# Four pieces instead of two begun tile by tile, with their low halves taken for both tiles at once

## The chip, the cores and the metric

One core of one Trainium2 chip runs the whole program. The metric is the device time of one execution in microseconds. Three runs of the kernel before gave a median of 1691.17 us (1690.84 to 1694.19).

## The reference, cut to what matters

The program computes three transformer layers over 256 tokens of width 1024, in float32. Three places in it matter here, and they have the same shape: a norm over the width, and right behind it a projection of all 256 normed tokens.

```
# layer 1, second half: PEER (product-key experts)
xn = rmsnorm(h, norm2_g)
q  = (xn @ w_q).reshape(n_tok, 8, 2, 128)         # 16 pieces of 128 columns
sc = einsum("thpk,hpnk->thpn", q, sub_keys)       # scores against 128 keys, then top 16 ...

# layers 2 and 3, second half: feed-forward with a short convolution (D_FF = 2816 = 22 chunks of 128)
h  = layer_norm(DEEPNORM_ALPHA * h + y, ln1_g, ln1_b)
gate, up = split(h @ w_in, 2)
gate = conv3(gate, conv_w) + conv_b
f  = (silu(gate) * up) @ w_out
```

## The kernel before, in words

**Numbers in two parts.** TensorE (PE) multiplies in a rounded 32-bit format. Each float32 operand is split: the high half is the value rounded by a copy on ACT, the low half is what is left, by a subtraction on DVE (`take_high` L807, `take_low` L1709 for a weight piece of 128x1024; L826 or L830 and L1722 or L1733 for the activations). A product is high x high + high x low + low x high.

**Pieces.** A projection of the normed tokens is cut into pieces of 128 output columns. A piece has 8 weight blocks of 128x128, one per 128 features (`k`). The result stands transposed, 128 columns by 256 tokens, in one PSUM bank of 512 columns. Weight pieces pass through a ring of four slots: SP loads `raw`, ACT makes `high`, DVE makes `low`, and PE frees the slot (`slot_done`).

**Three ways to do one piece.** `project_in` (L1244): three matmuls of 256 columns per `k` (L1240 to L1242), the sum complete in 256 PSUM columns. `project_in_halves` (L1256): the high weights against `[xh | xl]` as one matmul of 512 columns (L1260), then the low weights against `xh`, 256 columns (L1262); the two 256-column halves of the bank must be added later. `project_in_tile` (L1265): the same for one tile of 128 tokens; the high weights with 256 columns (L1273), the low weights with 128 columns (L1274). Two tiles make a piece, 32 matmuls.

**The norm and the projection meet.** The token tiles (0 and 1, 128 tokens each) leave the norm one after the other on DVE. `turn` (L1224) transposes a tile by 128x128 blocks (L1230), four blocks to a quarter; quarters 0 and 1 are tile 0, quarters 2 and 3 are tile 1, and quarter `n` lands in bank `4 + n`. ACT reads a quarter into `xh`, DVE makes `xl` from the bank and `xh` and raises `xT_ready`. `turn` of tile 0 is followed by `keep_warm` matmuls (L1236). Then, at all three places, PE's order is: piece 0 tile 0, `turn` of quarters 2 and 3, piece 1 tile 0, piece 0 tile 1, piece 1 tile 1. Each `k % 4 == 0` waits for its quarter. Behind that come two more pieces as a whole: queries 2 and 3 by `project_in` (L1352), or the gate and up pieces of chunk 1 by `project_in_halves` (`gate_and_up` L1674).

**What follows in the queries.** DVE adds the halves of queries 0 and 1 (L1967), then makes `xf` (L1971); ACT copies queries 2 and 3 out (L920). PE computes the scores of the four queries (L1361, 16 matmuls, banks 0 and 1), in order of the queries, then expert blocks (L1373).

**What follows in a feed-forward.** For chunk 0: ACT copies the gate's low-half sum (L1187), DVE adds the other half and does the convolution (L2395 to L2398), ACT applies Silu (L1190, after loading its table), ACT and DVE bring the `up` piece (L1192, L2405), DVE multiplies (L2407), ACT and DVE split the product into `yh` and `yl` (L1198, L1722). In between, both engines split weight pieces for the ring (`ahead`). PE then multiplies by the output weights (`project_out`, L1290 to L1294), which waits for `hid_low`, the signal of `yl`. In DVE's written order, `layer_norm` (L1794) ends with the low halves of quarters 2 and 3 and, behind them, the low halves of the two weight pieces of chunk 1 (`take_low`, L1812); only then comes chunk 0's `hidden`. The high halves of these two pieces are made early, ahead of tile 0's quarters (`norm`, L798). For the queries the order is the same: quarters 2 and 3 (L1961), then the low halves of queries 2 and 3.

Everything is in the written order of each engine; nothing is planned at run time.

## Time and profile before

| | |
|---|---|
| median of three runs | 1691.17 us |
| the profiled execution's own time | 1693.71 us |
| its span, first to last instruction | 1691.9 us |
| PE, DVE, ACT busy | 98%, 77%, 55% of the span |
| mean granted PE clock | 0.997 |
| from the first matmul of the four pieces to what follows them, queries | 206.68 to 221.61 us |
| the same, first feed-forward | 1172.78 to 1187.71 us |

The share of busy time says that PE is hardly ever without work in the long run; but PE's ends are modelled, and a busy PE isn't PE at its peak, so costs below are taken as distances between starts. A timeline row gives the start, the duration, the engine, the line, how many instructions were merged into it, and in brackets how long the engine had been idle and what released it.

### The profile page before, as it was taken

What the parts mean: (1) busy time and instruction counts of PE and PEld (TensorE: products, weight loads), DVE (VectorE), ACT (ScalarE), POOL (GpSimd) and SP (SyncE); (2) the same over time, 40 slices, a digit from 0 to 9 for tenths busy, and PEclk for the clock granted to TensorE, in tenths of its full rate; (3) what the DMA queues carried; (4) which work ended last, traced back from release to release, by engine and by line L of the source; (5) the groups of instructions that cost most, each with busy time, mean ns of one, the idle gap of its engine ahead of it and who ended that gap; (6) DMA issues with size and microseconds to landing.
All of it is one profiled execution on the core that took longest, in us unless ns stands there. A gap on an engine that the chain in (4) does not pass through costs nothing.

```text
span 1691.9 us, 28956 instructions
## 1 busy us (share of the span) xinstructions
PE 1664.5 (98%) x10092; PEld 1472.5 (87%) x10092; DVE 1303.5 (77%) x2467; ACT 933.1 (55%) x1633; POOL 107.3 (6%) x92
## 2 busy tenths in 40 slices
PE   7999999999999999999999999999999999999998
PEld 7999899999998888888888888897888888888886
DVE  7888789989997666666666666687877866687777
ACT  5666632268875444444444545575555545655554
POOL 0000000035550000000000000020000000000000
PEclk9999999999999999999999999999999999999999
DMA  6556733523336555555555556545666645256563
GB/s 217 180 180 198 247 132 135 193 78 114 115 107 213 189 188 187 186 187 188 186 189 193 188 196 236 166 135 173 193 190 187 200 137 161 89 192 189 190 188 111
DMA packets 84313, 292.96 MB, mean 173 GB/s; under 512 B 11664, under 2 KB 13456, under 8 KB 83856
## 3 DMA queue, kind: packets, MB, share of 16 engines
q1 hardware_dynamic: 82656, 286.54, 52.3%
q10 hardware_dynamic: 1584, 5.45, 1.0%
q8 instruction: 45, 0.74, 0.2%
q14 instruction: 28, 0.23, 0.0%
HBM read 289.33 MB, written 2.10 MB: 172 GB/s over the span
## 4 chain that ended last, share of the span: by engine, by line
PE 86%; issue 7%; DVE 4%; DMA 1%; ACT 1%; POOL 0%; SPq 0%; POOLq 0%; DVEq 0%; ACTq 0%
PE ps L1260 16%; PE ps L1290 10%; PE ps L1292 9%; PE ps L1294 9%; PE ps L1262 8%; PE ps L1240 7%; PE ps L1241 7%; PE ps L1242 7%; PE ps L1373 5%; PE ps L1398 3%; PE ps L1273 1%; DMA raw<-in_v_tab 1%; DVE low L1712 1%; DVE held_low L1712 0%; DVE arena L1781 0%
## 5 line engine op out<-in xcount | busy, mean ns | idle before, releaser
L1712 DVE TENSOR_TENSOR low<-raw,high 128x1024 fp32r<-128x1024 f32 x493 | 592.5, 1209 | 191.8 <-ACT high L814 184.9
L814 ACT ACTIVATE high<-raw 128x1024 fp32r<-128x1024 f32 x493 | 513.8, 1046 | 312.7 <-PE ps L1294 136.3
L1260 PE MATMUL ps<-x_parts,high 128*128 128x512 f32 x1216 | 432.7, 397 | 0.0
L1262 PE MATMUL ps<-x_parts,low 128*128 128x256 f32 x1216 | 341.0, 280 | 0.0
L1240 PE MATMUL ps<-x_parts,low 128*128 128x256 f32 x1104 | 317.4, 287 | 2.4 <-DVE x_parts L1733 1.9
L1242 PE MATMUL ps<-x_parts,high 128*128 128x256 f32 x1104 | 312.3, 283 | 0.0
L1241 PE MATMUL ps<-x_parts,high 128*128 128x256 f32 x1104 | 312.2, 283 | 0.0
L1260 PEld LDWEIGHTS ps<-x_parts,high 128*128 128x128 f32 x1216 | 228.4, 188 | 55.0
L1262 PEld LDWEIGHTS ps<-x_parts,low 128*128 128x128 f32 x1216 | 229.5, 189 | 4.0
L1240 PEld LDWEIGHTS ps<-x_parts,low 128*128 128x128 f32 x1104 | 211.5, 192 | 4.8 <-issue 2.3
L1241 PEld LDWEIGHTS ps<-x_parts,high 128*128 128x128 f32 x1104 | 211.7, 192 | 0.2
L1242 PEld LDWEIGHTS ps<-x_parts,high 128*128 128x128 f32 x1104 | 211.5, 192 | 0.0
L1290 PE MATMUL ps<-high,yl 128*128 128x512 f32 x640 | 199.9, 393 | 1.0 <-DVE yl L1722 1.0
L1292 PE MATMUL ps<-low,yh 128*128 128x512 f32 x640 | 198.9, 392 | 0.0
L1294 PE MATMUL ps<-high,yh 128*128 128x512 f32 x640 | 197.3, 389 | 0.0
L1292 PEld LDWEIGHTS ps<-low,yh 128*128 128x128 f32 x640 | 120.1, 188 | 27.6
L1294 PEld LDWEIGHTS ps<-high,yh 128*128 128x128 f32 x640 | 120.1, 188 | 27.0
L1290 PEld LDWEIGHTS ps<-high,yl 128*128 128x128 f32 x640 | 112.8, 188 | 23.6 <-DVE yl L1722 1.9
L762 POOL TENSOR_SCALAR h_tok<-consts,yh,spare 128x128 f32<-128x128 f32 x64 | 87.7, 1377 | 208.3 <-ACT yh L954 149.8
L751 POOL TENSOR_TENSOR stats<-stats 128x1 f32<-128x1 f32 x14 | 7.9, 565 | 1283.0 <-DVE stats L1753 1283.0
L1373 PE MATMUL ps<-arena 128*128 128x256 f32 x384 | 83.5, 379 | 0.0
L1373 PEld LDWEIGHTS ps<-arena 128*128 128x128 f32 x384 | 72.7, 190 | 9.7
(343 smaller groups left out, 2032.5 us busy)
## 6 DMA issues: line engine op xcount, KB each, us to landing
raw<-in_v_tab SPq DMA_DIRECT2D x128, 512.0 KB, 4.2
raw<-in_u_tab SPq DMA_DIRECT2D x104, 512.0 KB, 4.3
raw<-in_ffn_in SPq DMA_DIRECT2D x88, 512.0 KB, 4.0
raw<-in_w_mix SPq DMA_DIRECT2D x56, 512.0 KB, 4.5
raw<-in_ffn_out SPq DMA_DIRECT2D x44, 512.0 KB, 3.5
arena<-in_u_tab SPq DMA_DIRECT2D x24, 512.0 KB, 3.5
raw<-in_w_query SPq DMA_DIRECT2D x16, 512.0 KB, 5.3
raw<-in_diff_qk SPq DMA_DIRECT2D x16, 512.0 KB, 4.3
```

What stands on the lines that cost most here:

```text
L762: pool.tensor_scalar(one_hot_w[n % 2][:, 3 * PARTS:4 * PARTS], iota, sel_j[:, t:t + 1], weight[:, t:t + 1], ALU.is_equal, ALU.mult).then_i ...
L814: a.activation(w_high(p, 0, n), cols(raw, p, 0, n), ACT.Copy).then_inc(slot_high[p.slot], 1)
L1240: pe.matmul(dst, left[1], right[0], start=start, stop=False)
L1241: pe.matmul(dst, left[0], right[1], start=False, stop=False)
L1242: return pe.matmul(dst, left[0], right[0], start=False, stop=stop)
L1260: pe.matmul(bank(b).rearrange("p (h t) -> p h t", h=2), cols(high, p, k * PARTS, PARTS), both[:, :, k, :], start=(k == 0), stop=False)
L1262: ins = pe.matmul(bank(b, 0, SEQ), cols(low, p, k * PARTS, PARTS), chunk_of(xh, k), start=False, stop=(k == KC - 1))
L1290: pe.matmul(bank(2 * t + half), src_low[:, xs], w_high(p, half * HALF, HALF), start=first, stop=False)
L1292: pe.matmul(bank(2 * t + half), src_high[:, xs], w_low(p, half * HALF, HALF), start=False, stop=False)
L1294: ins = pe.matmul(bank(2 * t + half), src_high[:, xs], w_high(p, half * HALF, HALF), start=False, stop=stop)
L1373: ins = pe.matmul(bank(4 + early % 4, 0, SEQ), early_u[early % 4][:, k * PARTS:(k + 1) * PARTS], chunk_of(xf, k), start=(k == 0), stop=(k ...
L1712: v.tensor_tensor(w_low(p, 0, n), cols(raw, p, 0, n), w_high(p, 0, n).bitcast(F32), ALU.subtract).then_inc(slot_low[p.slot], 1)
```

## The change

At the three places, four pieces (queries 0 to 3; gate 0, up 0, gate 1, up 1) are begun by tile with their high weights alone. For tile 0, the high weights of all four pieces run (`project_high_tile`, 8 matmuls of 256 columns each); then PE transposes tile 1; then for each piece the high weights run for tile 1 and the low weights for both tiles at once (`project_low`, 8 matmuls of 256 columns). A piece is now 24 matmuls of 256 columns. Its bank is laid out as `project_in_halves` has it: high sum of both tiles in one half, the other products' in the other. The high matmul of a tile therefore writes two runs of 128 PSUM columns that lie 256 apart, and the first one of the bank (tile 0) carries `start`.

Since banks 4 to 7 are all in use by then, tile 1's quarters are transposed into banks 0 and 1, whose contents the norm has read. The first piece needs only its high half at first. Queries 2 and 3, too, are now summed by DVE (behind `xf`), not copied by ACT. `gate_and_up(1)` is gone from the first step of the feed-forward.

```diff
+        def turned_bank(k, n):
+            return bank(n - 2 if k in (1, 4, 6) and n >= 2 else 4 + n)
...
-                    if it >= 1 or q >= 2:
+                    if it >= 1:
                         a.activation(qs[:, q * SEQ:(q + 1) * SEQ], bank(4 + q, 0, SEQ), ACT.Copy).then_inc(q_ready, 1)
...
-            def project_in_tile(p, b, t, k_turn):
-                pe.wait_ge(slot_low[p.slot], p.count)
-                dst = by_tile_and_half(b)[:, t]
+            def project_high_tile(p, b, t, k_turn):
+                pe.wait_ge(slot_high[p.slot], p.count)
                 ts = slice(t * PARTS, (t + 1) * PARTS)
+                dst = bank(b).rearrange("p (h t) -> p h t", h=2)[:, :, ts]
                 for k in range(KC):
                     if k % 4 == 0:
                         pe.wait_ge(xT_ready, 4 * k_turn + 2 * t + k // 4 + 1)
-                    pe.matmul(dst, cols(high, p, k * PARTS, PARTS), both[:, :, k, ts], start=(k == 0), stop=False)
-                    ins = pe.matmul(dst[:, 0], cols(low, p, k * PARTS, PARTS), both[:, 0, k, ts], start=False, stop=(k == KC - 1))
-                if t == TB - 1:
-                    ins.then_inc(slot_done[p.slot], 1)
+                    pe.matmul(dst, cols(high, p, k * PARTS, PARTS), both[:, :, k, ts], start=(k == 0 and t == 0), stop=False)
+
+            def project_low(p, b):
+                pe.wait_ge(slot_low[p.slot], p.count)
+                for k in range(KC):
+                    ins = pe.matmul(bank(b, 0, SEQ), cols(low, p, k * PARTS, PARTS), chunk_of(xh, k), start=False, stop=(k == KC - 1))
+                ins.then_inc(slot_done[p.slot], 1)
+
+            def project_four(pieces, src, norm, k_turn):
+                for n, p in enumerate(pieces):
+                    project_high_tile(p, 4 + n, 0, k_turn)
+                turn(src, norm, (2, 3), k_turn)
+                for n, p in enumerate(pieces):
+                    project_high_tile(p, 4 + n, 1, k_turn)
+                    project_low(p, 4 + n)
...
             keep_warm(6, 7)
-            project_in_tile(Piece("query", 0), 4, 0, 1)
-            turn(tmp, 1, (2, 3))
-            project_in_tile(Piece("query", 1), 5, 0, 1)
-            project_in_tile(Piece("query", 0), 4, 1, 1)
-            project_in_tile(Piece("query", 1), 5, 1, 1)
+            project_four([Piece("query", n) for n in range(4)], tmp, 1, 1)
...
-                project_in_tile(piece_gate(l, 0), 4, 0, k_turn)
-                turn(h_tok, 3 + 2 * l, (2, 3))
-                project_in_tile(piece_up(l, 0), 5, 0, k_turn)
-                project_in_tile(piece_gate(l, 0), 4, 1, k_turn)
-                project_in_tile(piece_up(l, 0), 5, 1, k_turn)
+                project_four([piece(l, n) for n in range(2) for piece in (piece_gate, piece_up)], h_tok, 3 + 2 * l, k_turn)
...
                 def step(n, it):
-                    if n + 1 < FF_CHUNKS:
-                        if not (opening(it) and n == 0):
-                            pe.wait_ge(s["hid_ready"], it * 4 + n)
+                    if n + 1 < FF_CHUNKS and not (opening(it) and n == 0):
+                        pe.wait_ge(s["hid_ready"], it * 4 + n)
                         gate_and_up(n + 1, it)
...
-            for q in range(2):
+            for q in range(4):
+                if q == 2:
+                    v.wait_ge(xT_ready, 8)
+                    v.tensor_tensor(xf, xh[:, :].bitcast(F32), xl[:, :].bitcast(F32), ALU.add).then_inc(xf_ready, 1)
                 p = Piece("query", q)
                 v.wait_ge(slot_done[p.slot], p.done)
-                v.tensor_reduce(tiles_of(qs[:, q * SEQ:(q + 1) * SEQ]), by_tile_and_half(4 + q).rearrange("p t h n -> p t n h"),
-                                AX.X, ALU.add).then_inc(q_summed, 1)
-            v.wait_ge(xT_ready, 8)
-            v.tensor_tensor(xf, xh[:, :].bitcast(F32), xl[:, :].bitcast(F32), ALU.add).then_inc(xf_ready, 1)
+                v.tensor_reduce(qs[:, q * SEQ:(q + 1) * SEQ], halves(4 + q), AX.X, ALU.add).then_inc(q_summed, 1)
```

## Rows read from the trace of the kernel before

**Rows 1.** busy time of each engine (the page, part 1)

```profile
PE 1664.5 (98%) x10092; PEld 1472.5 (87%) x10092; DVE 1303.5 (77%) x2467; ACT 933.1 (55%) x1633; POOL 107.3 (6%) x92
```

**Rows 2.** the chain that ended last, by engine (the page, part 4)

```profile
PE 86%; issue 7%; DVE 4%; DMA 1%; ACT 1%; POOL 0%; SPq 0%; POOLq 0%; DVEq 0%; ACTq 0%
```

**Rows 3.** timeline of PE, queries: start us, us, engine line op out<-in xcount [idle]

```profile
206.68 0.36 PE L1273 MATMUL ps<-x_parts,high 128*128 128x256 f32 x1 [0.35 <-DVE x_parts L1733]
...
207.96 0.39 PE L1273 MATMUL ps<-x_parts,high 128*128 128x256 f32 x1 [0.17 <-DVE x_parts L1733]
...
208.94 1.05 PE L1230 MATMUL ps<-consts,arena 128*128 128x128 f32 x8
...
212.03 0.36 PE L1273 MATMUL ps<-x_parts,high 128*128 128x256 f32 x1 [0.26 <-DVE x_parts L1733]
...
212.98 0.38 PE L1273 MATMUL ps<-x_parts,high 128*128 128x256 f32 x1
...
215.81 0.33 PE L1240 MATMUL ps<-x_parts,low 128*128 128x256 f32 x1
...
221.61 1.95 PE L1361 MATMUL ps<-arena 128*128 128x128 f32 x16
...
223.39 0.81 PE L1373 MATMUL ps<-arena 128*128 128x256 f32 x3
```

**Rows 4.** timeline of DVE, queries, the second tile's lows

```profile
210.76 2.16 DVE L1733 SCALAR_TENSOR_TENSOR x_parts<-ps,params,x_parts 128x128 fp32r<-128x128 f32 x8 [2.07 <-ACT x_parts L830]
```

**Rows 5.** timeline of PE, first feed-forward

```profile
1172.78 0.36 PE L1273 MATMUL ps<-x_parts,high 128*128 128x256 f32 x1 [0.17 <-DVE x_parts L1722]
...
1174.54 0.38 PE L1273 MATMUL ps<-x_parts,high 128*128 128x256 f32 x1 [0.66 <-DVE x_parts L1722]
...
1175.52 1.25 PE L1230 MATMUL ps<-consts,h_tok 128*128 128x128 f32 x8
...
1176.52 0.36 PE L1273 MATMUL ps<-x_parts,high 128*128 128x256 f32 x1
...
1182.10 0.45 PE L1260 MATMUL ps<-x_parts,high 128*128 128x512 f32 x1
...
1187.71 0.62 PE L1290 MATMUL ps<-high,yl 128*128 128x512 f32 x2
```

**Rows 6.** timeline of DVE, first feed-forward

```profile
1176.80 1.32 DVE L1722 TENSOR_TENSOR x_parts<-ps,x_parts 128x512 fp32r<-128x512 f32 x2 [0.75 <-ACT x_parts L826]
...
1178.04 2.35 DVE L1712 TENSOR_TENSOR low<-raw,high 128x1024 fp32r<-128x1024 f32 x2
...
1180.86 0.42 DVE L2395 TENSOR_TENSOR arena<-arena,ps 128x256 f32<-128x256 f32 x1 [0.40 <-ACT arena L1187]
...
1185.90 0.42 DVE L1722 TENSOR_TENSOR yl<-arena,yh 128x256 fp32r<-128x256 f32 x1
```

**Rows 7.** timeline of ACT, first feed-forward

```profile
1180.45 0.39 ACT L1187 ACTIVATE arena<-ps 128x256 f32<-128x256 f32 x1 [3.04 <-PE ps L1274]
```

**Rows 8.** timeline of PE, second feed-forward

```profile
1498.12 0.39 PE L1273 MATMUL ps<-x_parts,high 128*128 128x256 f32 x1 [0.66 <-DVE x_parts L1722]
...
1499.09 1.24 PE L1230 MATMUL ps<-consts,h_tok 128*128 128x128 f32 x8
...
1511.28 0.62 PE L1290 MATMUL ps<-high,yl 128*128 128x512 f32 x2
```

**Rows 9.** timeline of DVE, second feed-forward

```profile
1504.43 0.42 DVE L2395 TENSOR_TENSOR arena<-arena,ps 128x256 f32<-128x256 f32 x1 [0.39 <-ACT arena L1187]
...
1509.55 0.42 DVE L1722 TENSOR_TENSOR yl<-arena,yh 128x256 fp32r<-128x256 f32 x1
```

**Rows 10.** stretches: busy us (count) of PE, PEld, DVE, ACT, POOL, then PEclk

```profile
1370.00:1373.00 3.00, 3.00 (x30) 3.00 (x29) 0.00 (x0) 0.00 (x0) 0.00 (x0) 1.00 0.33 134
1373.00:1377.00 4.00, 4.00 (x14) 3.22 (x14) 0.69 (x1) 1.42 (x2) 0.00 (x0) 0.57 0.53 165
...
1494.00:1499.00 5.00, 3.73 (x29) 3.23 (x28) 4.82 (x12) 2.44 (x4) 0.55 (x1) 1.00 0.00 0
```

More of the change, by code:

```diff
@@ L825, in evacuate_turned @@
                     if gain is None:
-                        ins = a.activation(turned_part(xh, n), bank(4 + n).rearrange("p (c t) -> p c t", c=4), ACT.Copy)
+                        ins = a.activation(turned_part(xh, n), turned_bank(k, n).rearrange("p (c t) -> p c t", c=4), ACT.Copy)
                     else:
@@ L829, in evacuate_turned @@
                             c = 4 * (n % 2) + i
-                            ins = a.activation(turned_part(xh, n)[:, i], bank(4 + n, i * PARTS, PARTS), ACT.Copy,
+                            ins = a.activation(turned_part(xh, n)[:, i], turned_bank(k, n)[:, i * PARTS:(i + 1) * PARTS], ACT.Copy,
                                                scale=params[:, c * NP + gain:c * NP + gain + 1])
@@ L1186, in hidden @@
                     a.wait_ge(slot_done[piece_gate(l, n, it).slot], piece_gate(l, n, it).done)
-                    a.activation(tiles_of(gate_sum[e]), half_of(4 + 2 * e, 1, n, it), ACT.Copy).then_inc(s["gate_half"], 1)
+                    a.activation(tiles_of(gate_sum[e]), half_of(4 + 2 * e, 1), ACT.Copy).then_inc(s["gate_half"], 1)
                     ahead(piece_gate(l, n, it))
@@ L1191, in hidden @@
                     a.wait_ge(slot_done[piece_up(l, n, it).slot], piece_up(l, n, it).done)
-                    a.activation(tiles_of(up_sum[e]), half_of(5 + 2 * e, 1, n, it), ACT.Copy).then_inc(s["up_half"], 1)
+                    a.activation(tiles_of(up_sum[e]), half_of(5 + 2 * e, 1), ACT.Copy).then_inc(s["up_half"], 1)
                     ahead(piece_up(l, n, it))
@@ L1223, in _, with turn @@
         def _(pe):
-            def turn(src, norm, quarters):
+            def turn(src, norm, quarters, k_turn=0):
                 for n in quarters:
@@ L1229, in turn @@
                         c = 4 * n + i
-                        ins = pe.transpose(bank(4 + n, i * PARTS, PARTS), src[:, c * PARTS:(c + 1) * PARTS], ident)
+                        ins = pe.transpose(turned_bank(k_turn, n)[:, i * PARTS:(i + 1) * PARTS], src[:, c * PARTS:(c + 1) * PARTS], ident)
                     ins.then_inc(turned, 1)
@@ L1348, in _ @@
             for it in range(4):
-                for q in range(0 if it else 2, 4):
-                    if it >= 1:
-                        pe.wait_ge(early_gelu, early - 4 + q + 1)
+                for q in range(0 if it else 4, 4):
+                    pe.wait_ge(early_gelu, early - 4 + q + 1)
                     project_in(Piece("query", 4 * it + q), bank(4 + q, 0, SEQ))
@@ L1355, in _ @@
                 for q in range(4):
-                    if it == 0 and q < 2:
+                    if it == 0:
                         pe.wait_ge(q_summed, q + 1)
                     else:
-                        pe.wait_ge(q_ready, 4 * it + q - 1)
+                        pe.wait_ge(q_ready, 4 * it + q - 3)
                     for t in range(TB):
@@ L2394, in hidden @@
                     v.wait_ge(s["gate_half"], it * 4 + (n + 1))
-                    link(v.tensor_tensor(tiles_of(gate), tiles_of(gate), half_of(4 + 2 * e, 0, n, it), ALU.add))
+                    link(v.tensor_tensor(tiles_of(gate), tiles_of(gate), half_of(4 + 2 * e, 0), ALU.add))
                     link(v.tensor_scalar(conv[e], gate, p[:, 2:3], p[:, 3:4], ALU.mult, ALU.add))
@@ L2404, in hidden @@
                     v.wait_ge(s["up_half"], it * 4 + (n + 1))
-                    link(v.tensor_tensor(tiles_of(up), tiles_of(up), half_of(5 + 2 * e, 0, n, it), ALU.add))
+                    link(v.tensor_tensor(tiles_of(up), tiles_of(up), half_of(5 + 2 * e, 0), ALU.add))
                     v.wait_ge(s["silu_ready"], it * 4 + (n + 1))
```

10 lines of the change are left out of this document (3 added, 7 removed).

## The prediction

> **What bounds the kernel now.** I read the page's busy times first: PE is busy for 98% of the span, DVE for 77% [rows 1]. The chain that ended last says the same from the other end: 86% of it is PE, 4% DVE [rows 2]. So PE's time is the program's time, and a microsecond that PE gains or loses at one of the three changed places comes out at the end, as long as whatever follows isn't waiting for something else. I then read the timelines at the three places, PE first and DVE and ACT beside it. What the reader is to see there is that these are the few places where PE does wait: at each, PE stops until DVE has finished a quarter. In the first feed-forward it begins at 1172.78, runs four pairs (k 0 to 3) and stands until 1174.54 for quarter 1 [rows 5]; in the queries the same two starts are 206.68 and 207.96 [rows 3]. The work behind these waits is what the change reorders, so both must be counted: PE's work, and what covers the norm's second tile.
>
> **Prices of a matmul.** In the queries 48 matmuls of 256 columns lie between 215.81 and 221.61: 0.121 us each; the 16 score matmuls of 128 columns take 221.61 to 223.39: 0.111 each [rows 3]. So a matmul of 128 columns costs hardly less than one of 256. In the first feed-forward the last 24 pairs (256 + 128 columns) of `project_in_tile` take 1176.52 to 1182.10, 0.2325 a pair, which leaves 0.1215 for the 256 columns; 16 pairs of 512 + 256 columns take 1182.10 to 1187.71, 0.351 a pair [rows 5]. I use 0.1205 for every 256-column matmul of the new order.
>
> **Part 1, PE's work falls.** Before, per feed-forward: 2 pieces x 16 pairs x 0.2325 = 7.44, and 2 whole pieces 5.61: 13.05 us. After: 4 x 24 x 0.1205 = 11.57. That is 1.5 us less per feed-forward; in the queries, where the other two pieces took 5.80, it is 13.24 - 11.57 = 1.7 less. All three together: 4.6 us. If nothing else moved, that would be the gain.
>
> **Part 2, the first tile's wait grows.** Quarter 1 is ready when DVE has made it, which nothing here moves. Ahead of it PE has now 4 matmuls (0.48) instead of 4 pairs (0.93). So k 4 starts at the same 1174.54, and 0.45 of each gain goes into that wait. The same holds for 207.96 and, in the second feed-forward, 1498.12 [rows 3, 5, 8].
>
> **Part 3, the transposes move back, and nothing covers them.** Before, tile 1 was transposed right behind piece 0's tile 0, and piece 1's tile 0 (8 pairs, 1.86 us) ran while ACT and DVE read the quarters. Now the transposes stand behind all four pieces' tile 0, and the next thing in PE's order needs their result. From k 4 to the transposes: 28 matmuls, 3.37 us.
>
> In the first feed-forward they start at 1174.54 + 3.37 = 1177.91. Before, DVE began quarter 2 1.28 us after the first transpose (1175.52 to 1176.80) and had both quarters after 2.60 [rows 5, 6]; half of DVE's 1.32 is quarter 2, so 1.94, and from there to PE's start about 0.15, as in the queries (DVE's first four of eight end near 211.84, PE starts at 212.03 [rows 3, 4]). PE starts tile 1 at 1180.00 and k 4 at 1177.91 + 2.60 + 0.15 = 1180.66. The 8 transposes themselves need some 0.9 to 1.0, so PE stands for about 1.1 us and again for 0.2. From k 4 on 60 matmuls are left, 7.23 us: PE is through at 1187.89. Before, it was at 1187.71. The whole 1.5 us is spent: 0.45 in part 2, 1.3 here.
>
> In the queries the quarters take longer, since ACT and DVE read them block by block: PE started tile 1 3.09 us after the transposes and k 4 4.04 after (208.94, 212.03, 212.98) [rows 3]. New: k 4 of tile 0 at 207.96, transposes at 211.33, tile 1 at 214.42, its k 4 at 215.37, end at 222.60. Before, 221.61. The score matmuls of queries 0 to 2 (12, 1.33 us) cover DVE's sum of query 3, so the scores end at 224.38 instead of 223.39: **0.99 us later**. The wait for tile 1 is over 2 us there, 1.7 of gain against 0.45 + some 2.2. The second tile's wait is some 0.9 longer than in a feed-forward, which is why the queries lose on PE alone.
>
> The second feed-forward repeats the first: k 4 at 1498.12, transposes at 1501.49 (before, 1499.09), k 4 of tile 1 at 1504.24, through at 1511.47 (before, 1511.28) [rows 8].
>
> **Part 4, chunk 0 is finished later, and the output projection waits for it.** Before, `hid_low` (end of DVE's L1722) came at 1185.90 + 0.42 = 1186.32 against PE's 1187.71: 1.4 us of slack [rows 5, 6]. Now gate 0 ends at 1180.66 + 12 x 0.1205 = 1182.11, ACT takes it 0.2 later, and DVE's L2395 could follow 0.41 behind ACT, as 1180.45 and 1180.86 show [rows 6, 7]: 1182.72. But DVE has quarters 2 and 3 until 1180.51 now, and in its written order the two low halves for chunk 1 come next: 2.27 us from L1712's start to `hidden`'s first instruction (1178.04 to 1180.31, L2393 being just ahead of L2395's 1180.86). So DVE is there at 1182.80. Both say the same, 1.94 us later than 1180.86. Everything from there to L1722 is one chain with the same ring work between its links, so `hid_low` comes at 1186.32 + 1.94 = 1188.26, and PE's output projection at 1188.41, **0.70 later** than 1187.71. In the second feed-forward the same steps give DVE's L2395 at 1506.38 instead of 1504.43, `hid_low` at 1511.92 and PE at 1512.07 instead of 1511.28: **0.79 later** [rows 8, 9]. The chain could partly be caught up (ACT's table load and its weight splits don't all shift), at most down to PE's own 0.18 and 0.19; it could also be later by one more weight split, 1.2 us, if one slips ahead of a link. I take the shift as it is worked out. Once the output projection runs, it and the next chunk's two pieces (5.6 us by themselves) stand before the next `hid_low` is needed, so nothing more is lost.
>
> **What costs nothing.** The two ACT copies of queries (0.4 us each) become DVE sums of 0.7; DVE is done with `xf` before query 3 ends, and waits. The ring's loads for queries 6 and 7 start later by the 2.4 us by which their slots' low halves do, but PE needs them only behind four expert blocks of 3.5 us. Banks 0 and 1 are read out before tile 1's norm is done, so the transposes there wait for nothing new. Waiting for the high half only saves nothing, since the first piece's low half lay ready.
>
> **Sum.** 0.99 + 0.70 + 0.79 = 2.5 us more. The profiled execution took 1693.71 us with a span of 1691.9; it would be 1696.2 with a span of 1694.4. It lies 2.5 us above the median of the runs, 1691.17, so against that median I predict 1693.7. What a measurement can tell from no change is about 0.2%, 3.4 us.
>
> **A rule against the change.** The new high matmul writes two runs of 128 PSUM columns instead of one of 256. No row here shows a matmul that writes in two runs; the one of two runs read (L1273's activations) costs no more than one. The price is bounded from below by nothing at 0.1205, from above by the pace of a matmul twice as wide, 0.351 - 0.121 = 0.230 [rows 3, 5]: 0.11 x 64 x 3 = 21 us. I take nothing, since the rows of two runs read are nearest. The Trainium skill, "PSUM — Partial Sum Buffer", Specifications (TRN2), says that any non-contiguous access pattern slows matmuls significantly; by it the kernel would be slower by up to that sum, and it is the third rival.
>
> **Rivals.**
> 1. *PE's own order decides, chunk 0 isn't late.* Part 4 fails: ACT and DVE catch up within PE's four pieces. The slack of 1.4 us speaks for it, the serial chain against it. Then 0.99 + 0.18 + 0.19 = 1.4: 1692.5.
> 2. *PE's clock falls in the new waits.* In the queries PE would work for about 1.5 of the 4 us from 211.33 on. Rows show the clock fall to 0.57 over 4 us (1373 to 1377) behind a stretch where PE stood for 1.1 us and then ran only 32-column matmuls, and they show it stay at 1.00 with PE busy for 3.73 of 5 us around the second feed-forward's waits [rows 10]. One fall costs 4 x 0.43 = 1.7: 1695.4; at all three places, 1698.8. The Trainium skill, "TensorE: Matmul & The Clock Gate", Part 1, has idleness bring back the slow clock and names nothing between its two states; the 0.57 is then a mean over both.
> 3. *Writing in two runs is slow.* Up to 1691.17 + 2.5 + 21 = 1715.
> 4. *Faster: the second tile is covered.* If the quarters of tile 1 were read within the transposes' own 1.0 us, only part 2's 0.45 of each place would be lost: 4.6 - 3 x 0.45 = 3.3 faster, or 1687.9. Its point is whether PE's tile 1 starts within 1.0 us of the first transpose. The rows have DVE only begin after 1.28, so it would take another order of ACT and DVE than the written one.
>
> **How the numbers follow.** The forecast has 50%; rival 1 17%, rival 2 15%, rival 3 4%, rival 4 10%, and 4% is left for what I don't see. The forecast's own range is 1692.5 to 1695.5. Over 1694.6 counts as slower by 0.2%: a quarter of the forecast (12), nearly all of rival 2 (13), rival 3 (4) and 1 of the unseen: 30%. Under 1687.8 counts as faster: rival 4 stands right at that bound and has 6 of its 10 below it, and 2 of the unseen: 8%. The rest, 62%, is within 0.2%. The range takes in the forecast, rival 1 with a microsecond of scatter below it, and one to two falls of the clock: 1690.0 to 1697.5.
>
> **What would show it right or wrong.** Right: k 4 of tile 0 at the same distance from the norm as before; four pieces' tile 0 in 3.4 us behind it; PE idle about 1.1 us behind the transposes in each feed-forward and over 2 us in the queries, released by DVE's `x_parts`; the output projection released by DVE's `yl` with PE idle for some 0.5 us. Wrong in price: a pitch of the high matmuls other than 0.12. Wrong in step: PE at L1290 not waiting (rival 1), a granted clock under 1 near the waits (rival 2), or tile 1 starting right behind its transposes (rival 4).

## The result and the profile after

The changed kernel takes 1696.83 us (median of 11 runs, 1693.98 to 1697.55); the kernel before, on the same chip and in turn with it, takes 1693.49 (11 runs, 1690.84 to 1695.69). The ratio is 1.0017 with a 95% interval of 1.0009 to 1.0025: 2.9 us slower, between 1.5 and 4.2 (the medians themselves lie 3.3 apart), which is inside the 0.2% that I had called no change. The predicted step was +2.5. The predicted time of 1693.7 stands 3.1 below the measured one, and 2.3 of these are the kernel before itself: the three runs shown had a median of 1691.17, the eleven have 1693.49. The profiled execution took 1697.00 with a span of 1695.2, against 1693.71 and 1691.9. One execution of `e9_gate_first` further down took 5634.93 us, over three times as long as its others, and is left out of its median and ratio.

The page of the kernel after, its head, the busy times and the chain by engine, against [rows 1, 2]:

```profile
span 1695.2 us, 28936 instructions
...
PE 1663.5 (98%) x10076; PEld 1471.9 (87%) x10076; DVE 1304.7 (77%) x2469; ACT 931.9 (55%) x1631; POOL 106.5 (6%) x92
...
PE 85%; issue 7%; DVE 4%; ACT 2%; DMA 1%; POOL 0%; SPq 0%; POOLq 0%; DVEq 0%; ACTq 0%
```

PE still sets the end. The page can't tell more of a change of 3 us, so the timelines of the three places have to. This is PE in the queries (start, us, engine, line, operation, count, and in brackets the idle time ahead of it with what ended it), the answer to [rows 3]:

```profile
208.01 0.71 PE L1271 MATMUL ps<-x_parts,high 128*128 128x256 f32 x4 [0.35 <-DVE x_parts L1734]
209.29 3.62 PE L1271 MATMUL ps<-x_parts,high 128*128 128x256 f32 x28 [0.57 <-DVE x_parts L1734]
212.75 1.04 PE L1228 MATMUL ps<-consts,arena 128*128 128x128 f32 x8
215.84 2.16 PE L1271 MATMUL ps<-x_parts,high 128*128 128x256 f32 x8 [2.05 <-DVE x_parts L1734]
217.80 1.83 PE L1277 MATMUL ps<-x_parts,low 128*128 128x256 f32 x8
219.47 1.11 PE L1271 MATMUL ps<-x_parts,high 128*128 128x256 f32 x8
220.42 1.12 PE L1277 MATMUL ps<-x_parts,low 128*128 128x256 f32 x8
...
225.22 1.95 PE L1367 MATMUL ps<-arena 128*128 128x128 f32 x16
```

L1271 is the high half by tile, L1228 the transposes, L1277 the low half, L1367 the scores. k 4 of tile 0 starts at 209.29, the transposes 3.46 later (worked out: 3.37), tile 1 another 3.09 later (3.09), with the wait of 2.05 us that was to be over 2. Then comes a thing the forecast did not have in its sum: 16 matmuls from 215.84 to 219.47 take 3.63 us, where the next 16 take 1.91. (The next 16 wait for nothing. The fair comparison is the same 16 at full clock, with their wait for the tile's second quarter, in `e1_queries` below: 2.47, so the price is 1.16.) The stretches of the same kernel (busy us and count of each engine, then the granted clock) name it:

```profile
212.00:215.84 3.84, 1.79 (x17) 1.58 (x15) 1.28 (x5) 2.18 (x8) 0.00 (x0) 1.00 0.42 171
215.84:219.40 3.56, 3.56 (x16) 3.37 (x17) 3.15 (x6) 0.00 (x0) 0.00 (x0) 0.52 0.09 30
219.40:225.20 5.80, 5.80 (x50) 5.80 (x50) 4.18 (x4) 3.18 (x3) 0.00 (x0) 1.00 0.43 165
```

Behind a stretch in which PE worked for 1.79 of 3.84 us the clock stood at 0.52, near the lower of its two levels (1.2 and 2.4 GHz), and came back while PE was busy. This is rival 2 at one place, beside the forecast and not in its stead.

In the first feed-forward the clock stayed at 1.00. PE there, the answer to [rows 5]:

```profile
1177.89 3.62 PE L1271 MATMUL ps<-x_parts,high 128*128 128x256 f32 x28 [1.05 <-DVE x_parts L1723]
1181.35 1.04 PE L1228 MATMUL ps<-consts,h_tok 128*128 128x128 f32 x8
1183.45 1.25 PE L1271 MATMUL ps<-x_parts,high 128*128 128x256 f32 x8 [1.07 <-DVE x_parts L1723]
...
1190.30 1.12 PE L1277 MATMUL ps<-x_parts,low 128*128 128x256 f32 x8
1191.63 0.72 PE L1301 MATMUL ps<-high,yl 128*128 128x512 f32 x2 [0.21 <-DVE yl L1723]
```

And DVE beside it, the answer to [rows 6]:

```profile
1182.61 1.29 DVE L1723 TENSOR_TENSOR x_parts<-ps,x_parts 128x512 fp32r<-128x512 f32 x2 [3.21 <-ACT x_parts L824]
1183.82 2.35 DVE L1713 TENSOR_TENSOR low<-raw,high 128x1024 fp32r<-128x1024 f32 x2
...
1186.16 0.41 DVE L2395 TENSOR_TENSOR arena<-arena,ps 128x256 f32<-128x256 f32 x1
...
1191.16 0.42 DVE L1723 TENSOR_TENSOR yl<-arena,yh 128x256 fp32r<-128x256 f32 x1
```

Here is part 4 as it was worked out: DVE goes without a wait from the two low halves of chunk 1 (L1713) to L2395, which stands 8.27 us behind k 4 of tile 0 (8.26), `yl` at 1191.16, and PE's output projection standing until 1191.63, released by it. From k 4 to the output projection it is 13.74 us, before 13.17.

All of the 3.3 us between the two spans, by stretches (after less before): up to the queries +1.33, which has nothing of the change in it; the queries +2.28; from there to the first feed-forward -0.26; its opening +0.57; to the second -1.40; its opening +0.58; the rest +0.20. The change's own part is 3.4, of which the clock has 1.2.

### The profile page after: what moved, and what is told of

It reads as the page before. It is cut to its first block, busy times and chain, and to the rows that moved or that the text cites. A ratio compares the mean times of both kernels' runs of the same rounds, so it can differ in the third digit from the quotient of the medians.

```text
span 1695.2 us, 28936 instructions
## 1 busy us (share of the span) xinstructions
PE 1663.5 (98%) x10076; PEld 1471.9 (87%) x10076; DVE 1304.7 (77%) x2469; ACT 931.9 (55%) x1631; POOL 106.5 (6%) x92
## 4 chain that ended last, share of the span: by engine, by line
PE 85%; issue 7%; DVE 4%; ACT 2%; DMA 1%; POOL 0%; SPq 0%; POOLq 0%; DVEq 0%; ACTq 0%
PE ps L1258 16%; PE ps L1301 10%; PE ps L1303 9%; PE ps L1305 9%; PE ps L1260 8%; PE ps L1238 7%; PE ps L1239 7%; PE ps L1240 7%; PE ps L1379 5%; PE ps L1404 3%; PE ps L1271 1%; DVE low L1713 1%; DMA raw<-in_v_tab 1%; DVE held_low L1713 0%; DVE arena L1782 0%
## 5 line engine op out<-in xcount | busy, mean ns | idle before, releaser
L1713 DVE TENSOR_TENSOR low<-raw,high 128x1024 fp32r<-128x1024 f32 x493 | 592.8, 1209 | 186.0 <-ACT high L812 182.7
L1258 PE MATMUL ps<-x_parts,high 128*128 128x512 f32 x1184 | 421.4, 397 | 0.0
L1260 PE MATMUL ps<-x_parts,low 128*128 128x256 f32 x1184 | 332.2, 281 | 0.0
L1238 PE MATMUL ps<-x_parts,low 128*128 128x256 f32 x1088 | 313.7, 288 | 1.8 <-DVE x_parts L1734 1.3
L1239 PE MATMUL ps<-x_parts,high 128*128 128x256 f32 x1088 | 308.6, 284 | 0.0
L1240 PE MATMUL ps<-x_parts,high 128*128 128x256 f32 x1088 | 308.5, 284 | 0.0
L1258 PEld LDWEIGHTS ps<-x_parts,high 128*128 128x128 f32 x1184 | 222.4, 188 | 53.7
L1260 PEld LDWEIGHTS ps<-x_parts,low 128*128 128x128 f32 x1184 | 223.5, 189 | 4.0
L1238 PEld LDWEIGHTS ps<-x_parts,low 128*128 128x128 f32 x1088 | 209.4, 192 | 4.3 <-issue 2.3
L1239 PEld LDWEIGHTS ps<-x_parts,high 128*128 128x128 f32 x1088 | 209.6, 193 | 0.2
L1240 PEld LDWEIGHTS ps<-x_parts,high 128*128 128x128 f32 x1088 | 209.3, 192 | 0.0
```

Source lines behind the costliest of these rows:

```text
L1238: pe.matmul(dst, left[1], right[0], start=start, stop=False)
L1239: pe.matmul(dst, left[0], right[1], start=False, stop=False)
L1240: return pe.matmul(dst, left[0], right[0], start=False, stop=stop)
L1258: pe.matmul(bank(b).rearrange("p (h t) -> p h t", h=2), cols(high, p, k * PARTS, PARTS), both[:, :, k, :], start=(k == 0), stop=False)
L1260: ins = pe.matmul(bank(b, 0, SEQ), cols(low, p, k * PARTS, PARTS), chunk_of(xh, k), start=False, stop=(k == KC - 1))
L1713: v.tensor_tensor(w_low(p, 0, n), cols(raw, p, 0, n), w_high(p, 0, n).bitcast(F32), ALU.subtract).then_inc(slot_low[p.slot], 1)
```

## The experiments

One distance serves for all of them: from k 4 of tile 0 to the first instruction behind the changed block (the scores in the queries, the output projection in the feed-forwards). It leaves out the scatter of the other 1650 us. For kernels in which k 4 no longer waits, 1.28 us (queries) or 1.76 (feed-forwards) behind the first matmul of tile 0 stands for it, as in the kernel before. Each ratio is to executions of the kernel before that were taken in turn with that kernel; the medians of different rows can't be set against each other as closely.

| kernel | queries | FF 1 | FF 2 | median us (runs) | ratio to before, 95% |
|---|---|---|---|---|---|
| before | 13.65 | 13.17 | 13.16 | 1693.49 (11) | |
| after | 15.93 c | 13.74 | 13.74 | 1696.83 (11) | 1.0017 (1.0009 to 1.0025) |
| e1_queries | 14.77 | 13.18 | 13.27 | 1693.96 (10) | 1.0009 (1.0000 to 1.0018) |
| e2_ffns | 13.65 | 13.73 | 13.80 | 1694.71 (10) | 1.0009 (1.0000 to 1.0018) |
| e3_turn_after_one | 12.01 | 14.34 c | 12.97 | 1692.28 (11) | 0.9988 (0.9979 to 0.9997) |
| e4_warm | 14.76 | 13.73 | 13.74 | 1695.80 (10) | 1.0015 (1.0006 to 1.0025) |
| c1_after_again | 15.98 c | 15.24 c | 15.22 c | 1699.86 (1) | |
| f1_no_warm | 16.22 c | 13.74 | 13.75 | 1697.17 (1) | |
| e6_three | 12.01 | 12.56 | 12.56 | 1691.12 (10) | 0.9990 (0.9980 to 0.9999) |
| e8_halves | 11.60 | 11.89 | 11.89 | 1689.48 (11) | 0.9976 (0.9967 to 0.9985) |
| c2_after_third | 14.76 | 13.74 | 13.73 | 1694.25 (1) | |
| c3_before_again | 13.64 | 13.17 | 13.27 | 1694.92 (1) | |
| f2_warm_all | 14.77 | 13.74 | 13.72 | 1694.94 (11) | 1.0010 (1.0001 to 1.0018) |
| e9_gate_first | 11.61 | 11.46 | 11.47 | 1689.10 (5) | 0.9966 (0.9953 to 0.9979) |

The c marks a place at which the granted clock fell to about half in the profiled execution.

**e1_queries: the change in the queries alone.** The old `project_in_tile` and its bank layout are put back for the feed-forwards.

```diff
-            return bank(n - 2 if k in (1, 4, 6) and n >= 2 else 4 + n)
+            return bank(n - 2 if k == 1 and n >= 2 else 4 + n)
...
-                project_four([piece(l, n) for n in range(2) for piece in (piece_gate, piece_up)], h_tok, 3 + 2 * l, k_turn)
+                project_in_tile(piece_gate(l, 0), 4, 0, k_turn)
+                turn(h_tok, 3 + 2 * l, (2, 3))
+                project_in_tile(piece_up(l, 0), 5, 0, k_turn)
+                project_in_tile(piece_gate(l, 0), 4, 1, k_turn)
+                project_in_tile(piece_up(l, 0), 5, 1, k_turn)
...
```

> The change in the queries alone; both feed-forwards as before. Measure: the distance from PE's k 4 of tile 0 (first L-of-the-high-matmul start behind the first wait) to what follows the four pieces. Before: 13.65 us in the queries, 13.17 and 13.16 in the feed-forwards; changed kernel 15.93, 13.74, 13.74. Theory (each place pays for its own uncovered transposes, and nothing is carried from one to another): queries 15.9, feed-forwards 13.2, kernel 2.3 us slower than before. Rival (the places interact, or the loss is in what follows, such as the scores or the ring's loads): another value at either, or a total that isn't 2.3.

**e2_ffns: the change in the feed-forwards alone**, the same the other way round; queries 2 and 3 run whole and are copied by ACT again.

```diff
-            project_four([Piece("query", n) for n in range(4)], tmp, 1, 1)
+            project_in_tile(Piece("query", 0), 4, 0, 1)
+            turn(tmp, 1, (2, 3))
+            project_in_tile(Piece("query", 1), 5, 0, 1)
+            project_in_tile(Piece("query", 0), 4, 1, 1)
+            project_in_tile(Piece("query", 1), 5, 1, 1)
...
```

> The change in the two feed-forwards alone; the queries as before. Theory: queries 13.65 us from k 4 to the scores, feed-forwards 13.74 each to the output projection, 1.1 us slower than before in all. Rival (the feed-forwards' loss hangs on the shift that the queries hand them, through the ring's phase): 13.2 in the feed-forwards and no loss.

Each half costs 0.09% (0.00 to 0.18), together the 0.17% of the whole. These intervals are too wide to say more; that the places don't act on each other, and that none of them gains, is shown by the distances. At each the distance grows where the change is and stands where it isn't: +1.12 in the queries of e1 (+0.99 was worked out), with the clock at 1.00 throughout, and +0.56 and +0.64 in the feed-forwards of e2 (+0.70 and +0.79). I had expected 15.9 in e1's queries, as in the profile after, and 14.77 was a miss: the difference is the clock's. The queries of e1, PE's timeline, are the forecast's own picture, without the fall of the clock:

```profile
207.89 3.62 PE L1277 MATMUL ps<-x_parts,high 128*128 128x256 f32 x28 [0.57 <-DVE x_parts L1758]
211.35 1.04 PE L1234 MATMUL ps<-consts,arena 128*128 128x128 f32 x8
214.43 0.71 PE L1277 MATMUL ps<-x_parts,high 128*128 128x256 f32 x4 [2.05 <-DVE x_parts L1758]
215.38 0.73 PE L1277 MATMUL ps<-x_parts,high 128*128 128x256 f32 x4 [0.23 <-DVE x_parts L1758]
215.95 1.11 PE L1283 MATMUL ps<-x_parts,low 128*128 128x256 f32 x8
216.90 1.12 PE L1277 MATMUL ps<-x_parts,high 128*128 128x256 f32 x8
217.86 1.12 PE L1283 MATMUL ps<-x_parts,low 128*128 128x256 f32 x8
...
222.66 1.95 PE L1386 MATMUL ps<-arena 128*128 128x128 f32 x16
```

The eight high matmuls from 216.90 (two runs of 128 columns in PSUM) take 0.96 us, as the eight low ones from 215.95 (one run of 256) take 0.95. The price of writing in two runs is nothing, so rival 3 is refuted.

**e3_turn_after_one: the transposes behind piece 0's tile 0**, as before the change; three pieces' tile 0 then stand behind them.

```diff
                 for n, p in enumerate(pieces):
                     project_high_tile(p, 4 + n, 0, k_turn)
-                turn(src, norm, (2, 3), k_turn)
+                    if n == 0:
+                        turn(src, norm, (2, 3), k_turn)
```

> The changed kernel with one edit: tile 1's transposes stand behind piece 0's tile 0 again, ahead of tile 0 of pieces 1 to 3, which are 24 matmuls or 2.9 us. Theory (the loss is that nothing covers the transposes): in the feed-forwards the quarters need 2.1 us and are covered; PE doesn't stop for tile 1; gate 0 is complete 1.4 us sooner and the output projection starts 12.2 to 12.4 us behind k 4 (before 13.17, changed 13.74). In the queries the quarters need 3.1 and 4.0 us against 2.9 + 0.5: PE stops for at most 0.3, the clock stays, 12.0 to 12.3 us from k 4 to the scores (before 13.65, changed 15.93). Kernel 3.1 to 3.6 us faster than before, about 1690. Rival (the work itself costs more than counted: two-run writes, or the high halves of four pieces in a row): the wait goes, but the feed-forwards stay at 13.2 or more.

The queries went from 14.77 to 12.01, 2.76 us, and PE waits for nothing behind k 4. This is the test of part 3: the order of the matmuls is the changed kernel's, only the cover is back, and the kernel is 0.12% (0.03 to 0.21) faster than before instead of slower. That is 2.0 us, where I had expected 3.1 to 3.6. The feed-forwards were a miss, in two ways. In the first the clock fell. In the second, at full clock, it was 12.97 and not 12.2 to 12.4; PE there:

```profile
1497.23 0.74 PE L1271 MATMUL ps<-x_parts,high 128*128 128x256 f32 x4 [1.05 <-DVE x_parts L1724]
1498.13 1.32 PE L1228 MATMUL ps<-consts,h_tok 128*128 128x128 f32 x8 [0.16 <-DVE h_tok L1792]
1499.20 4.08 PE L1271 MATMUL ps<-x_parts,high 128*128 128x256 f32 x32
...
1508.88 1.12 PE L1277 MATMUL ps<-x_parts,low 128*128 128x256 f32 x8
1510.20 0.73 PE L1302 MATMUL ps<-high,yl 128*128 128x512 f32 x2 [0.21 <-DVE yl L1724]
```

The transposes are now so early that they wait for the second tile's norm and run with it; and at the end PE still waits for `yl`. Chunk 0 bounds this feed-forward by now: part 4's chain, not PE.

**e4_warm: 16 matmuls on constants in the queries' long wait.**

```diff
                 turn(src, norm, (2, 3), k_turn)
+                if k_turn == 1:
+                    keep_warm(2, 8)
```

> The changed kernel with 16 warming matmuls (128 columns, into bank 2, which is read by then) behind tile 1's transposes in the queries alone: 1.9 us of work laid into the 2.05 us wait. In the changed kernel the first 12 matmuls behind that wait took 0.21 to 0.24 us each instead of 0.12, with a granted clock of 0.52 from 215.8 to 219.4. Theory (the wait lets the clock fall): the clock stays at 1.00, these matmuls take 0.12, the scores start 1.2 us sooner: 14.7 us from k 4 (15.93 without). Rival (they are slow for another reason, such as ACT and DVE reading PSUM or writing x_parts at the same time): they stay slow, 15.9 or more.

The number came as expected (14.76, clock 1.00), and by itself it says little: e1 had the same 14.77 with nothing in the wait, and the kernel's ratio of 1.0015 is hardly another than 1.0017. That called for repeats of the same kernel.

**c1_after_again, c2_after_third: the changed kernel unaltered. c3_before_again: the kernel before unaltered.**

> The changed kernel once more, one profile. Theory (the clock falls behind the queries' wait in some executions only): 14.8 us from k 4 to the scores where the clock stays, 15.9 where it falls; everything else as in the first profile. Rival (the slow 3.6 us belong to this program's queries): 15.9 again.

> The changed kernel, a third profile. So far its clock fell at one of the three places in the first profile and at all three in the second. Theory (the new waits let it fall in some executions): at least one fall in the three places, 1.2 us for each in the queries and 1.5 in a feed-forward. Rival (the second profile was an exception): none.

> The kernel before, a second profile. In the six places that still had the old order so far (three here, two and one in the kernels with half of the change) the clock stayed at 1.00. Theory: it stays again, 13.65, 13.17 and 13.16 us. Rival (the falls are as common in the old order): one or more of them 1.2 us longer with a granted clock under 1.

Here is the second part of the price. One and the same kernel had a fall at the queries (after), at all three places (c1), and at none (c2, where I had expected at least one). The first feed-forward of c1, PE's 28 matmuls from k 4 on:

```profile
1177.98 5.12 PE L1271 MATMUL ps<-x_parts,high 128*128 128x256 f32 x28 [1.05 <-DVE x_parts L1723]
```

The same row of c2:

```profile
1175.21 3.62 PE L1271 MATMUL ps<-x_parts,high 128*128 128x256 f32 x28 [1.05 <-DVE x_parts L1723]
```

That is 1.5 us for the fall. The stretches of c1 there (PE, PEld, DVE, ACT, POOL, clock) have it at half speed for about 3 us right behind the first tile's wait:

```profile
1176.00:1178.00 2.00, 0.72 (x5) 0.55 (x5) 1.93 (x4) 0.75 (x2) 0.56 (x1) 1.00 0.00 0
1178.00:1180.00 2.00, 2.00 (x12) 2.00 (x13) 1.42 (x2) 0.00 (x0) 0.00 (x0) 0.69 0.03 8
1180.00:1182.00 2.00, 2.00 (x11) 2.00 (x11) 0.00 (x0) 0.00 (x0) 0.00 (x0) 0.50 0.00 0
1182.00:1184.00 2.00, 1.99 (x17) 1.74 (x15) 0.00 (x0) 0.41 (x1) 0.00 (x0) 0.96 0.00 0
```

Counted over all profiled executions, the new order with nothing added in its waits fell at 4 of 16 places: 2 of 4 in the queries, 2 of 12 in feed-forwards. The old order fell at 0 of 9. These are few, from seven profiled executions with the new order, three of them of one kernel; a difference of 4 of 16 against 0 of 9 can be chance.

All executions help here, not only those with a profile, since each has its mean granted clock on record, rounded to 0.001. The kernel before was run 71 times beside the experiments. Its mean time is 1692.5 us where the clock was 0.999 (22 executions), 1693.5 at 0.998 (32) and 1694.7 at 0.997 (17). So the clock falls elsewhere in the program too, as [rows 10] show, and a good part of the scatter is its. The changed kernel's 11 took 1695.1 (1), 1695.7 (5) and 1697.1 (5) at the same three clocks: at an equal clock the change costs 2.3 us in the mean, as much as the distances without a fall add up to. The mean clock is 0.9976 in the changed kernel and 0.9981 before. With 1.1 us for each 0.001 that is another 0.5 us, an estimate from these runs: less than the 1.1 of the counts that follow below, and uncertain by half, for each of the two kernels with half of the change has 0.9976 as well.

**f1_no_warm: without the matmuls on constants that stand ahead of the queries.**

```diff
-            keep_warm(6, 7)
             project_four([Piece("query", n) for n in range(4)], tmp, 1, 1)
```

> The changed kernel without the 14 warming matmuls ahead of the queries' four pieces: PE stands for 1.7 us more in front of them, nothing later depends on them. Theory (what PE did in the microseconds before decides on the clock): the clock falls in or ahead of the queries' pieces, and the distance from k 4 to the scores is 15.9 us or more, with a granted clock under 1. Rival (the fall has nothing to do with idle time): 14.8 with the clock at 1.00.

The clock fell earlier, at the first tile (0.54 and 0.60 in the two stretches of 2 us from 208.98), and the distance was 16.22. A fall at this spot in the queries was seen in no other profile, which speaks for the idle stretch ahead of it. It doesn't show it: this is one execution, and 2 of 4 queries with the warming matmuls in place had a fall too, further back.

**f2_warm_all: matmuls on constants in both waits at all three places.**

```diff
                 for k in range(KC):
+                    if k == 4 and t == 0 and b == 4:
+                        keep_warm(2, 2 if k_turn == 1 else 4)
...
                 turn(src, norm, (2, 3), k_turn)
+                keep_warm(2, 8 if k_turn == 1 else 4)
```

> The changed kernel with warming matmuls of 128 columns in both of its waits at all three places: 4 or 8 in the wait for quarter 1, 8 or 16 behind the transposes. They do no useful work and must not lengthen the waits. Theory (the falls come from the waits): no fall in the three places, 14.8 us in the queries and 13.75 in the feed-forwards, and the median 1 to 2 us under the changed kernel's 1696.8, with few executions above 1696. Rival (the falls have another cause): falls as before, the same median.

The distances are those of the changed kernel without a fall, so the added matmuls cost nothing. No place fell; but at 4 of 16, three places in a row stay without one in four cases of ten by chance alone. The highest of 11 runs is 1696.68, and the ratio went from 1.0017 to 1.0010. The difference, 1.2 us, is near what the counts give (queries 2/4 x 1.2, two feed-forwards 2/12 x 1.5 each: 1.1). But the two intervals overlap, so this supports the clock's share and doesn't prove its size. What is left, 0.10% or 1.7 us (0.01 to 0.18%), is in keeping with the forecast's mechanism (2.3 us by the distances).

**e6_three: in the feed-forwards only three pieces by tile, the fourth whole and last.**

```diff
-                for n, p in enumerate(pieces):
+                by_tile = pieces if k_turn == 1 else pieces[:3]
+                for n, p in enumerate(by_tile):
                     project_high_tile(p, 4 + n, 0, k_turn)
-                turn(src, norm, (2, 3), k_turn)
-                for n, p in enumerate(pieces):
+                    if n == 0:
+                        turn(src, norm, (2, 3), k_turn)
+                for n, p in enumerate(by_tile):
                     project_high_tile(p, 4 + n, 1, k_turn)
                     project_low(p, 4 + n)
+                if k_turn != 1:
+                    project_in_halves(pieces[3], 7)
```

> On top of the kernel with the transposes behind piece 0: in the feed-forwards only gate 0, up 0 and gate 1 are begun by tile, up 1 runs whole behind them. PE's work is the same (0.351 for a pair of 512 and 256 against 3 x 0.12), but gate 0 is complete 0.96 us sooner. Theory (in the feed-forwards what starts the output projection is chunk 0's chain, not PE): with the clock at 1.00 PE's wait for yl (0.2 to 0.36 us there) goes, and the distance from k 4 to the output projection falls from 12.97 to 12.6, no further, since PE's own work is then the bound. Rival (PE's work is the bound already): 12.97 stays. Queries 12.0 as before it.

The first feed-forward, PE's k 4 and the output projection:

```profile
1173.10 0.74 PE L1271 MATMUL ps<-x_parts,high 128*128 128x256 f32 x4 [1.05 <-DVE x_parts L1727]
...
1185.66 0.62 PE L1305 MATMUL ps<-high,yl 128*128 128x512 f32 x2
```

PE's own work is nearly the same: the whole piece is 8 x 0.351 = 2.81 us, by tile 24 x 0.120 = 2.88. In e3 PE was through 12.61 behind k 4 (1508.88 + 0.96 - 1497.23) and then stood until 12.97. Here it is through and goes on at 12.56, since 8 matmuls fewer stand ahead of chunk 0's gate: the wait for `yl` is gone. By the distances at full clock that is 0.8 us for both feed-forwards against e3; the kernels' times don't show it (0.9990 and 0.9988, with intervals that overlap almost wholly).

**e8_halves: both waits filled with the other pieces' first halves.** k 0 to 3 of all four pieces' tile 0 come first, then k 4 to 7 of all, with the transposes ahead of piece 0 (queries) or piece 2 (feed-forwards) in that second round. Tile 1 is begun with k 0 to 3 of two pieces. Quarters 0 and 1 go to banks 0 and 1.

```diff
+                first, second = range(KC // 2), range(KC // 2, KC)
+                turn_at = 0 if k_turn == 1 else 2
                 for n, p in enumerate(pieces):
-                    project_high_tile(p, 4 + n, 0, k_turn)
-                turn(src, norm, (2, 3), k_turn)
+                    project_high_tile(p, 4 + n, 0, k_turn, first)
                 for n, p in enumerate(pieces):
-                    project_high_tile(p, 4 + n, 1, k_turn)
+                    if n == turn_at:
+                        turn(src, norm, (2, 3), k_turn)
+                    project_high_tile(p, 4 + n, 0, k_turn, second)
+                for n in range(2):
+                    project_high_tile(pieces[n], 4 + n, 1, k_turn, first)
+                for n, p in enumerate(pieces):
+                    project_high_tile(p, 4 + n, 1, k_turn, second if n < 2 else range(KC))
                     project_low(p, 4 + n)
```

> The version that the theory asks for: both waits get work. All four pieces run k 0 to 3 of tile 0 ahead of k 4 to 7 (16 matmuls, 1.9 us, against the first tile's wait of 1.3 to 1.8), and the transposes stand between them, in the queries ahead of the first piece's k 4, in the feed-forwards ahead of the third's. Quarters 0 and 1 go to banks 0 and 1 too. Theory: counted from where the first k 4 started before (DVE's end of quarter 1), the queries take 11.5 us (before 13.65), the feed-forwards 11.3 to 11.8 (before 13.17), the clock doesn't fall, and the kernel is 4.5 to 5.5 us faster than before, 0.3%. Rival (the order of DVE and ACT, the lows of chunk 1 above all, sets the feed-forwards' pace by now): queries as said, feed-forwards at 12.3 or more.

The first feed-forward, PE's timeline:

```profile
1171.62 3.12 PE L1271 MATMUL ps<-x_parts,high 128*128 128x256 f32 x24 [0.17 <-DVE x_parts L1730]
1174.58 1.03 PE L1228 MATMUL ps<-consts,h_tok 128*128 128x128 f32 x8
1175.37 2.98 PE L1271 MATMUL ps<-x_parts,high 128*128 128x256 f32 x20
1178.18 1.12 PE L1277 MATMUL ps<-x_parts,low 128*128 128x256 f32 x8
...
1183.46 1.12 PE L1277 MATMUL ps<-x_parts,low 128*128 128x256 f32 x8
1185.27 0.73 PE L1308 MATMUL ps<-high,yl 128*128 128x512 f32 x2 [0.69 <-DVE yl L1730]
```

Part 2's wait of 1.05 us is gone as well. The distances are 11.60 and 11.89, the kernel 0.24% or 4.1 us faster than before (0.27% by the distances), a little less than the 4.5 to 5.5 expected. In the feed-forward PE now waits 0.69 at the end, and the 11.89 were a little over what I had expected (11.3 to 11.8): again chunk 0.

**e9_gate_first: e8, and in the feed-forwards piece 0 is finished before piece 1's tile 1 begins.**

```diff
-                for n in range(2):
+                ahead_of = 2 if k_turn == 1 else 0
+                for n in range(ahead_of):
                     project_high_tile(pieces[n], 4 + n, 1, k_turn, first)
...
-                    project_high_tile(p, 4 + n, 1, k_turn, second if n < 2 else range(KC))
+                    project_high_tile(p, 4 + n, 1, k_turn, second if n < ahead_of else range(KC))
```

> On top of the version with both waits filled: in the feed-forwards piece gate 0 finishes tile 1 and its low weights ahead of up 0's first half, so gate 0 is complete 0.3 to 0.5 us sooner, at the price of at most 0.2 us of waiting for quarter 3. Theory (chunk 0's chain starts the output projection there, PE waits 0.69 us for yl): the distance from the first matmul to the output projection in the second feed-forward falls from 13.65 to about 13.3, PE's wait to 0.2 or 0.3, 0.7 us in all. Rival (the chain's start is set by DVE's lows of chunk 1): 13.65 stays.

PE's timeline of the same place:

```profile
1171.88 3.12 PE L1271 MATMUL ps<-x_parts,high 128*128 128x256 f32 x24 [0.17 <-DVE x_parts L1731]
...
1178.02 1.11 PE L1277 MATMUL ps<-x_parts,low 128*128 128x256 f32 x8
...
1183.77 1.12 PE L1277 MATMUL ps<-x_parts,low 128*128 128x256 f32 x8
1185.10 0.73 PE L1309 MATMUL ps<-high,yl 128*128 128x512 f32 x2 [0.21 <-DVE yl L1731]
```

Gate 0's low half begins 6.14 us behind the first matmul, in e8 6.56, so 0.42 sooner; the output projection starts 0.43 sooner (13.22 from the first matmul, 13.3 expected). PE's own work is as long as before, 12.85 against 12.80 to the end of the last L1277. The chain moved, PE's work didn't, and the end moved with the chain: in this order it is chunk 0 that starts the output projection, by part 4's mechanism. DVE beside it:

```profile
1179.64 0.41 DVE L2403 TENSOR_TENSOR arena<-arena,ps 128x256 f32<-128x256 f32 x1
```

DVE stood for 0.29 us ahead of this instruction (L2402 there) in e8, and doesn't here: it comes straight from the low halves of chunk 1. So an even earlier gate 0 would gain nothing; the rival that the expectation names is what bounds the chain's start from here on. e9_gate_first is the fastest version: 0.34% faster than the kernel before (0.21 to 0.47%), 5.4 us by the distances. Its interval and that of e8 overlap.

## Why the prediction was right

**Prices and part 1.** 28 matmuls from k 4 to the transposes took 3.46 us (0.1236 each), 3.37 by 0.1205 each; where 8 stand alone they take 0.96 (0.120). The 0.09 wasn't followed further. In e1's queries the 96 matmuls take 0.48 + 3.46 + 0.48 + 7.28 = 11.70 us (11.57), 1.54 less than the 13.24 before. e3's queries are 1.64 us shorter than before, but that is a nearness by chance to the 1.7 of part 1: the distance leaves out the first four pairs, so only 1.09 of it is PE's work, and some 0.55 are waits that the old order had and e3 hasn't.

**Part 2.** The first tile's wait grew as said: 1.05 us in place of 0.66 in a feed-forward [rows 5], and k 4 stood at the same 1.76 us behind the first matmul. e8 filled this wait with others' k 0 to 3. The queries got 0.41 from that, the step from e3's 12.01 to 11.60, where 0.45 had been worked out.

**Part 3.** From the first transpose to tile 1: 2.10 us in the feed-forward (2.09) and 3.09 in the queries (3.09). PE's own end came 0.2 later in a feed-forward (0.18). In the queries the scores came 1.12 later at full clock (0.99); 0.09 of the 0.13 is the one above.

**Part 4.** The output projection was later by 0.57 and 0.58, where I had 0.70 and 0.79, and PE was idle for only 0.21 ahead of it. The head of the chain was right to 0.01 us. Of the 0.13, 0.04 were caught up between L2395 and `yl` (5.00 us against 5.04 in [rows 6]), and 0.10 are PE's start, 0.47 behind `yl`'s, where I had put 0.42 + 0.15. In the second feed-forward the same two are 0.12 (5.00 against 5.12, [rows 9]) and 0.10. Rival 1, that chunk 0 isn't late, is refuted by this wait, and by e9.

**The mis-sized term** is rival 2's. I had the clock as a case beside the forecast, with 15%, and 1.7 us for each fall. It is an additional price that comes in some executions: 1.2 in the queries and 1.5 in a feed-forward when it comes, by the counts some 1.1 us in the mean. By the mean clocks of all executions it is some 0.5. So the sum is 1.12 + 0.57 + 0.58 = 2.3 without a fall, 2.8 with the clock's share by the mean clocks and 3.4 with that by the counts, against 2.5 forecast and 2.9 (1.5 to 4.2) measured. That 2.5 came so close is in part luck: the queries were put 0.13 too low, the two feed-forwards 0.34 too high together, and the clock at nothing; and an interval of 2.7 us can't tell these sums apart. The rows pointed both ways: those of [rows 10] show one fall and one place without, and I took the second as the rule. What the Trainium skill, "TensorE: Matmul & The Clock Gate", Part 1, says of idleness bringing back the slow clock fits the places that fell, and not the twelve with the same waits that didn't; why the same 1 to 2 us of waiting bring it back in one execution and not in the next, no run here shows. The wait ahead of the first quarter doesn't sort them: it was 0.57 us in c1's first feed-forward and 0.17 in e3's, which both fell, and 0.60 in e3's second, which didn't.

The Trainium skill, "PSUM — Partial Sum Buffer", Specifications (TRN2), would have had the new matmuls slow. The measurement decides against it for this pattern: 0.120 us each in two runs as in one.

**Rival 4** was the one with something to build on. It would have had tile 1 covered by a faster ACT and DVE, for 3.3 us; from the first transpose to tile 1 it was 2.1 and 3.1 us and not 1.0, so it failed. e3 covers tile 1 by PE's own order instead (2.0 us faster than before by the ratio, 0.5 to 3.6), and e8 and e9 filled part 2's wait too (4.1 and 5.8).

## What to carry to other kernels

Where two groups of work take turns (transposes, then matmuls that need their result), the matmuls saved are worth nothing if the saving also takes the matmuls that stood in between: put the transposes where at least as much other work stands behind them as their round through ACT and DVE takes, here 2.1 and 3.1 us, and count this before the matmuls. Work that waits for half of its input can be cut at that half, and the other pieces' first halves put in the wait. Once PE's own time at such a place is down, look at who waits for the first finished piece, and finish that one first.

## What was not expected of the hardware

- The granted clock halves for about 3 us behind PE's waits of 1 to 2 us in some executions and not in others of the same kernel (4 of 16 places), and each time costs 1.2 to 1.5 us. A single profile can't tell such a price; the mean clock of many executions, set beside their times, comes nearer.
- Matmuls on constants in a wait cost nothing where PE would have stood, if they end before the wait does: 14.77 us with and without them, and at none of the four places that had them did the clock fall (which, at 4 of 16 without them, may be chance).
- A matmul that writes two runs of 128 PSUM columns, 256 apart, goes at the same 0.120 us as one of 256 in a row.
